# Expert tiles gather their rows by token number and add their outputs into a token-ordered sum

## What is computed

```
x = _layer_norm(DEEPNORM_ALPHA * x + mixed, ln_g[l, 0], ln_b[l, 0])
x = _layer_norm(DEEPNORM_ALPHA * x + grouped_moe(x, ...), ln_g[l, 1], ln_b[l, 1])

def grouped_moe(x, w_router, b_router, w_e_in, w_e_out):
    # best of 4 groups, then its 2 best experts of 4: expert (T, 2), weight (T, 2)
    flat_e = expert.reshape(-1)
    order = jnp.argsort(flat_e)
    tok = order // TOP_K
    h = lax.ragged_dot(xt[tok], w_e_in, group_sizes)      # 16 experts, 1024 -> 2 * 512
    h_gate, h_up = jnp.split(h, 2, axis=-1)
    y = lax.ragged_dot(jax.nn.silu(h_gate) * h_up, w_e_out, group_sizes)   # 512 -> 1024
    y = y * weight.reshape(-1)[order][:, None]
    return jnp.zeros_like(xt).at[tok].add(y)
```

## Time and profile before

| what | us |
|---|---|
| median of 3 runs (lowest, highest) | 3569.72 (3567.91, 3579.04) |
| span of the profiled execution, its own time | 3573.8 |
| layer 1: end of the mixer to the table | 1132 to 1255 |
| layer 1: table to the first product | 1255 to 1301 |
| layer 1: tile loop | 1301 to 1722 |
| layer 1: last eviction to the last bias | 1722 to 1802 |
| layer 2: the same four | 2910 to 3036, to 3082, to 3496, to 3569 |

### The profile page before, as it was taken

One profiled execution on the slowest core, in us unless ns is written; L12 is line 12 of the kernel. 1 busy time (PEld: TensorE's weight loads), 2 busy tenths in 40 slices (PEclk: granted clock), 3 DMA queues, 4 the chain that ended last, 5 costly groups with the idle time before them and its releaser, 6 DMA issues.

```text
span 3573.8 us, 47212 instructions
## 1 busy us (share of the span) xinstructions
PE 3068.0 (86%) x15514; PEld 1681.2 (47%) x15515; DVE 1576.8 (44%) x2553; ACT 1173.2 (33%) x1823; POOL 248.1 (7%) x146
## 2 busy tenths in 40 slices
PE   6899897899998749999378998968999986599992
PEld 4466555544444424544134666555444444244451
DVE  3333353423333348656633334534323323368666
ACT  3223302322221037656221233022222210367652
POOL 0000000000001240000400000000000012400005
PEclk8999896699999869999678997957999997799995
DMA  9200102021211079777511000020221120689764
GB/s 366 90 1 1 48 1 59 1 59 29 59 53 65 30 297 353 272 276 293 194 54 57 1 20 29 1 59 1 59 56 32 53 68 27 241 327 374 306 249 165
DMA packets 197713, 422.18 MB, mean 118 GB/s; under 512 B 13700, under 2 KB 99888, under 8 KB 196752
## 3 DMA queue, kind: packets, MB, share of 16 engines
q1 hardware_dynamic: 174112, 328.65, 26.2%
q10 hardware_dynamic: 13552, 55.58, 3.9%
q0 software_dynamic: 9920, 36.29, 2.8%
HBM read 352.31 MB, written 72.35 MB: 119 GB/s over the span
## 4 chain that ended last, share of the span: by engine, by line
PE 66%; issue 11%; DVE 7%; PEld 4%; ACT 3%; DMA 3%; POOL 2%; DVEq 1%; POOLq 1%; SPq 1%; PEldq 1%; ACTq 0%
PE PA L1724 14%; PE PB L1743 7%; PE PA L1394 6%; PE PA L1395 6%; PE PA L1396 6%; PE PB L1395 3%; PE PB L1394 3%; PE PB L1396 3%; PE PC L1375 2%; PE PB L1488 1%; PE PB L1594 1%; PE PD L1515 1%; PEld PA L1394 1%; POOLq L509 1%; POOL RC L510 1%
## 5 line engine op out<-in xcount | busy, mean ns | idle before, releaser
L1724 PE MATMUL PA<-XT,RA 128*128 128x512 f16 x2304 | 511.2, 382 | 36.7 <-DVE RA L879 33.0
L1724 PEld LDWEIGHTS PA<-XT,RA 128*128 128x128 f16 x2304 | 226.8, 99 | 303.4 <-issue 42.1
L879 DVE SCALAR_TENSOR_TENSOR XT<-OT,XT 128x1024 f16<-128x1024 f32 x256 | 300.1, 1245 | 105.8 <-ACT XT L770 105.8
L770 ACT ACTIVATE XT<-OT 128x1024 f16<-128x1024 f32 x256 | 247.7, 1045 | 150.1 <-DMA OT<-in_w_e_in_dram 108.0
L1394 PE MATMUL PA<-XT,W 128*128 128x512 f16 x704 | 268.7, 382 | 13.9 <-ACT WK L733 5.8
L1395 PE MATMUL PA<-XT,W 128*128 128x512 f16 x704 | 268.8, 382 | 0.0
L1396 PE MATMUL PA<-XT,W 128*128 128x512 f16 x704 | 268.5, 381 | 0.0
L1743 PE MATMUL PB<-W,WK 128*128 128x512 f16 x1152 | 260.1, 383 | 8.6 <-DVE W L879 5.7
L879 DVE SCALAR_TENSOR_TENSOR W<-W 128x512 f16<-128x512 f32 (+2 forms) x288 | 177.5, 659 | 171.7 <-ACT W L582 159.6
L1394 PE MATMUL PA<-W,XT 128*128 128x512 f16 (+1 forms) x640 | 237.7, 371 | 13.8 <-DVE W L879 12.8
L1395 PE MATMUL PA<-W,XT 128*128 128x512 f16 (+1 forms) x640 | 236.7, 370 | 0.0
(11 more groups left out here) (320 smaller groups left out, 4746.5 us busy)
## 6 DMA issues: line engine op xcount, KB each, us to landing
OT<-in_w_e_in_dram SPq DMA_DIRECT2D x256, 512.0 KB, 7.6
RA<-in_w_e_out_dram SPq DMA_DIRECT2D x128, 512.0 KB, 6.3
W<-in_w_in_dram SPq DMA_DIRECT2D x104, 512.0 KB, 6.2
RA<-rows SPq DMA_DIRECT2D x50, 512.0 KB, 5.4
rows<-WK ACTq DMA_DIRECT2D x48, 512.0 KB, 5.6
rows<-RA ACTq DMA_DIRECT2D x1, 16384.0 KB, 59.0
BR<-in_w_branch_dram SPq DMA_DIRECT2D x16, 512.0 KB, 6.9
W<-in_w_out_dram SPq DMA_DIRECT2D x16, 512.0 KB, 5.7
```

Of the source, the lines that this page charges most:

```text
L770: nc.scalar.activation(EIS[:, 0, k, :], WEI[:, k, :], ACT.Copy, scale=SW).then_inc(ei_hi, 1)
L879: return stt(dst, src, scale, high, ALU.mult, ALU.subtract)
L1724: q = mm(PA[:, half, :], ROWS[:, a, k * P:(k + 1) * P], EIS[:, b, k, half * HALF:(half + 1) * HALF], start=k == 0 and a + b == 0, stop=k = ...
```

## The change

The rows are no longer scattered to slots. Instead:

- SyncE stores each finished tile of `X1` to a token-ordered DRAM tensor `x1_rows`, whose last 128 rows are zero.
- Behind the table, VectorE and TensorE invert the slot numbers. For each of the 16 columns of slots, VectorE makes a one-hot of the rank in the tile (B) and of the tile, times token number and times weight (A); 16 float32 matmuls sum B-transposed times A. Out come `src_row` (for each row of each tile its token) and `row_wt` (its weight). Slots without a token point to padding rows.
- GpSimd gathers `ROW` of each tile by `src_row`, and for each tile adds the output rows, which ScalarE has scaled by `row_wt` at eviction, to `y_sum` by an accumulating indirect DMA. `y_sum` is in token order and is cleared at the end of the mixer by a DMA from `y_zero`, DRAM to DRAM, issued by GpSimd ahead of its first gain.
- SyncE's first weight load no longer stands behind the dispatch, and its loop holds weight loads only. After the last add it loads `y_sum` tile by tile, with four buffers.
- In the combine one VectorE instruction (`X1 * ALPHA + y`) takes the place of two, and GpSimd's alpha pass and gathers are gone.
- Small: `mem` is loaded by one DMA, the zeros written at the start are 9 + 1 tiles and not 32.

The diff, cut to its core (in order: GpSimd at the end of the mixer, GpSimd behind the table, ScalarE's eviction, VectorE and TensorE behind the table, VectorE in the combine):

```diff
+                    if t == 0:
+                        pool.wait_ge(zero_st, 32)
+                        pool.dma_start(y_sum, y_zero).then_inc(y_st, 16)
                     r = WK[:, (t % 2) * D:(t % 2 + 1) * D]
                     nc.gpsimd.tensor_tensor(r, r, lnp[0], ALU.mult)
...
-                for t in range(NT):
-                    for j in range(2):
-                        nc.gpsimd.indirect_dma_start(
-                            rows, bass.IndirectOffsetOnAxis(slots[:, j, t:t + 1], 0), X1[:, t, :], None
-                        ).then_inc(disp, 16)
-                pool.wait_ge(disp, at(disp, 2 * NT * 16))
-                for t in range(NT):
-                    nc.gpsimd.tensor_scalar(X1[:, t, :], X1[:, t, :], ALPHA, None, ALU.mult)
-                pool.wait_ge(y_st, (g0 + n_tiles + 1) * 16)
-                for t in range(NT):
-                    pool.wait_ge(y_used, at(y_used, t + 1))
-                    for j in range(2):
-                        nc.gpsimd.indirect_dma_start(
-                            OT[:, (2 * (t % 2) + j) * D:(2 * (t % 2) + j + 1) * D], None,
-                            rows, bass.IndirectOffsetOnAxis(slots[:, j, t:t + 1], 0)
-                        ).then_inc(y_ld[t % 2], 16)
+                def gather_tile(i):
+                    pool.wait_ge(row_tr, g0 + i + l)
+                    nc.gpsimd.tensor_copy(at_row[:, 0:1], src_row[:, bass.ds(i, 1)])
+                    pool.drain()
+                    gather(at_row[:, 0:1])
+                def add_rows(i):
+                    pool.wait_ge(y_ev, g0 + i + 2)
+                    nc.gpsimd.tensor_copy(at_row[:, 1:2], src_row[:, bass.ds(i, 1)])
+                    pool.drain()
+                    nc.gpsimd.indirect_dma_start(y_sum, bass.IndirectOffsetOnAxis(at_row[:, 1:2], 0), YROW, None,
+                                                 compute_op=ALU.add).then_inc(y_st, 16)
+                pool.wait_ge(x1_st, at(x1_st, NT * 16))
+                pool.wait_ge(inv_ok, at(inv_ok, 1))
+                gather(src_row[:, 0:1])
...
+                with pool.Fori(1, last) as i:
+                    gather_tile(i + 2)
+                    add_rows(i - 1)
+                add_rows(before_last)
+                add_rows(last)
...
-                    act.wait_ge(y_st, (g0 + i + 1) * 16)
-                    nc.scalar.activation(WK[:, 2048:3072], flat(PB), ACT.Copy, scale=UN).then_inc(y_ev, 1)
-                    act.drain()
-                    act.dma_start(rows[bass.ds(i * P, P), :], WK[:, 2048:3072]).then_inc(y_st, 16)
+                    act.wait_ge(y_st, (g0 + i) * 16 + (l + 1) * 16)
+                    nc.scalar.activation(YROW, flat(PB), ACT.Copy, scale=row_wt[:, bass.ds(i, 1)]).then_inc(y_ev, 1)
...
+                tt(A[:, :, TILES:2 * TILES], over(tile_f, TILES),
+                   co("iota128")[:, 0:TILES].unsqueeze(1).to_broadcast([P, 2 * NT, TILES]), ALU.is_equal)
+                tt(B, over(rank_f, P), co("iota128").unsqueeze(1).to_broadcast([P, 2 * NT, P]), ALU.is_equal)
+                tt(A[:, :, 0:TILES], A[:, :, TILES:2 * TILES], over(who, TILES), ALU.mult)
+                tt(A[:, :, TILES:2 * TILES], A[:, :, TILES:2 * TILES],
+                   over(m12[:, 2:4, :].rearrange("p j t -> p (j t)"), TILES), ALU.mult).then_inc(inv_a, 1)
+                v.wait_ge(inv_mm, at(inv_mm, 1))
+                ts(src_row[:, :], PC[:, 0, 0:TILES], co("tokid")[:, 0:1], 2.0 * T, ALU.add, ALU.add)
+                ts(row_wt[:, :], PC[:, 0, TILES:2 * TILES], UN, None, ALU.mult)
+                v.drain().then_inc(inv_ok, 1)
...
+                for i in range(2 * NT):
+                    q = mm(PC[:, 0, 0:2 * TILES], B[:, i, :], A[:, i, :], start=i == 0, stop=i == 2 * NT - 1)
+                q.then_inc(inv_mm, 1)
...
-                        stt(r, y1, m12[:, 2, t:t + 1], X1[:, t, :], ALU.mult, ALU.add)
-                        v.drain()
-                        stt(r, y2, m12[:, 3, t:t + 1], r, ALU.mult, ALU.add).then_inc(y_used, 1)
+                        stt(r, X1[:, t, :], ALPHA, OT[:, t % 4 * D:(t % 4 + 1) * D], ALU.mult, ALU.add
+                            ).then_inc(y_used, 1)
```

More of the change, by code:

```diff
@@ L107, in trunk @@
         mem_t = dram("mem_t", [P, 2 * KD * N_MEM], F16)
-        rows = dram("rows", [TILES * P, D])
+        x1_rows = dram("x1_rows", [T + P, D])
+        y_sum = dram("y_sum", [T + P, D])
+        y_zero = dram("y_zero", [T + P, D])
         keep_rate = dram("keep_rate", [LAYERS, BW])
@@ L210, in trunk @@
         par_ld = sem("par_ld", 6 * 16)
-        nat_ld = [sem(f"nat_ld{i}") for i in range(NT + MT)]
+        nat_ld = [sem(f"nat_ld{i}") for i in range(NT + 1)]
         bt_tr = sem("bt_tr", 1)
@@ L321, in trunk @@
         y_st = sem("y_st")
-        y_ld = [sem(f"y_ld{i}", 8 * 16) for i in range(2)]
+        y_ld = [sem(f"y_ld{i}", 2 * 16) for i in range(4)]
         y_used = sem("y_used", NT)
@@ L359, in _ @@
             sp.dma_start(CO[:, :], consts).then_inc(c_ld, 16)
[L360 to L365, removed]
+            for t in range(NT):
+                sp.dma_start(RC[:, t * D:(t + 1) * D], x[0, t * P:(t + 1) * P, :]).then_inc(nat_ld[t], 16)
+            sp.dma_start(OT[:, 0:MT * D].rearrange("p (t d) -> p t d", t=MT), mem[0].rearrange("(t p) d -> p t d", p=P)
+                         ).then_inc(nat_ld[NT], 16)
             sp.dma_start(hmask[:, :], chunk_mask).then_inc(misc_ld, 16)
@@ L419, in _ @@
                     sp.sem_inc(passed, 1)
-                for t in range(NT):
-                    sp.wait_ge(o_rd, at(o_rd, t + 1))
-                    sp.dma_start(xres[t % 2], out[0, t * P:(t + 1) * P, :]).then_inc(xr_ld[t % 2], 16)
+                for t in range(NT + 3):
+                    if t < NT:
+                        sp.wait_ge(o_rd, at(o_rd, t + 1))
+                        sp.dma_start(xres[t % 2], out[0, t * P:(t + 1) * P, :]).then_inc(xr_ld[t % 2], 16)
+                    if t >= 3:
+                        sp.wait_ge(o_x1, at(o_x1, t - 2))
+                        sp.dma_start(x1_rows[(t - 3) * P:(t - 2) * P, :], X1[:, t - 3, :]).then_inc(x1_st, 16)
                 sp.wait_ge(o_mm, at(o_mm, NT))
@@ L472, in _ @@
                 sp.dma_start(RA[:, 0:KD * N_MEM].bitcast(F16), mem_t).then_inc(mt_ld, 16)
+                sp.wait_ge(y_st, (g0 + last + 1) * 16 + (l + 1) * 16)
                 sp.sem_inc(passed, 1)
+                for t in range(NT):
+                    if t >= 4:
+                        sp.wait_ge(y_used, at(y_used, t - 3))
+                    sp.dma_start(OT[:, t % 4 * D:(t % 4 + 1) * D], y_sum[t * P:(t + 1) * P, :]).then_inc(y_ld[t % 4], 16)
             for i in range(4):
@@ L531, in _, with gather @@
-                for t in range(NT):
-                    pool.wait_ge(y_used, at(y_used, t + 1))
-                    pool.sem_inc(passed, 1)
-                    for j in range(2):
-                        nc.gpsimd.indirect_dma_start(
-                            OT[:, (2 * (t % 2) + j) * D:(2 * (t % 2) + j + 1) * D], None,
-                            rows, bass.IndirectOffsetOnAxis(slots[:, j, t:t + 1], 0)
-                        ).then_inc(y_ld[t % 2], 16)
-                    if t == 2:
-                        pool.wait_ge(ln2_ld, at(ln2_ld, 32))
-                    if t >= 2:
-                        gain(pool, l, t - 2)
+                def gather(column):
+                    nc.gpsimd.indirect_dma_start(ROW, None, x1_rows, bass.IndirectOffsetOnAxis(column, 0)
+                                                 ).then_inc(row_ld, 16)
@@ new lines, in _ @@
+                pool.sem_inc(passed, 1)
+                gather(src_row[:, 1:2])
+                pool.wait_ge(row_tr, g0 + (l + 2))
+                pool.sem_inc(passed, 1)
+                gather(src_row[:, 2:3])
+                with pool.Fori(1, last) as i:
[3 more added lines that the diff above has]
+                add_rows(last)
+                pool.wait_ge(ln2_ld, at(ln2_ld, 32))
+                for t in range(NT - 2):
+                    gain(pool, l, t)
@@ L1804, in constants @@
     put("ones", np.ones((P, P)))
[L1805 to L1807 removed]
     put("thr", np.tile(np.arange(8) * P, (P, 1)))
+    put("iota128", np.tile(np.arange(P), (P, 1)))
+    put("tokid", i[:, None] + P * np.arange(NT)[None, :] - T)
     return c, (same & (j_ <= i_)).astype(np.int32)
```

82 lines of the change are left out of this document (47 added, 35 removed).

## The result

| | median (lowest, highest), us | ratio to the kernel before, 95% interval |
|---|---|---|
| before | 3570.89 (3567.91, 3579.04), 4 runs | |
| after | 3551.65 (3550.95, 3556.59), 4 runs | 0.9947 [0.9933, 0.9961] |

The profiled execution's span is 3550.5 us, against 3573.8. The forecast, 3507 with a range of 3484 to 3545, gave the right sign and missed the size: about a third of the gain came. Each stage of a layer is cut here at the same marks, in the profiled executions: GpSimd's release at the mixer's end (its first gain pass, or the clear ahead of it), the cast of the table, the first and the last eviction of the tile loop, and VectorE's last scaling of the combine.

The account below looks back on a forecast made before the run. TensorE is two thirds of the chain, so only its idle stretches pay. Head 42.6, clear -1.4, loop -4, combine 3.5 and 22.2 sum to 62.9 off 3573.8: span 3510.9, median 3507 us, range 3484 to 3545.

Parts of the forecast that it names:

- the clear: Mixer's end: GpSimd's 4.7 MB DMA ahead of its first gain costs only its issue, 0.7 us a layer, 1.4 for both.
- the loop: Tile loop of both layers: a loss of 4 us in all, from the adds' extra bytes on full DMA engines.
- the start: Kernel start up to layer 1's GpSimd release: moved by 0; nothing costed for the zeros or the one mem load.
- the head: Table cast to first product: some 25.2 us against 46.5, a gain of 21.3 in each layer, 42.6.
- the combine: After the last eviction: first sum earlier by 3.4 and 0.1 us, then tiles in 45.0, gaining 13.5 and 8.7.
- Rival 4: Mixer's end: the clear holds GpSimd until it is copied, 2 x 19.1 us on TensorE's wait, 3545; chance 0.08.
- about 1.7, and its landing: Tile loop: an add needs 1.7 us for hand-over, index copy and issue, plus 8.0 landing: 9.7 of 15.85, hidden.
- the prediction's 1.28: Tile loop: an add moves 0.5 MB more than the store did, 1.28 us of the DMA engines at 410 GB/s.
- What would show the prediction wrong: ScalarE waiting for y_sum, weight chunks waited for in dense stretches beyond a few us, or the chain through the clear.
- the inversion's 7.06 us of matmuls: Head: 16 float32 matmuls, two weight loads of 0.22 us each, 7.0 us in all.
- the first weight DMA: Head: SyncE loads four registers first, so its first weight DMA is issued about 3 us after the cast.
- the hand-over: Last eviction's end to the combine's first sum: 13.6 us, from 1.7 + 8.0 for the add, 0.2, and 3.7 for the first load.

Follow-up runs that it names:

- run 2: Changed kernel, with a semaphore wait instead of the drain between GpSimd's first gain and bias passes, behind the clear: 3518.24 us.
- run 8: Kernel before, with GpSimd issuing a 4.7 MB DRAM copy to an unread buffer ahead of its first gain pass in each layer: 3601.74 us.
- run 3: Changed kernel with semaphore waits for both the tile loop's two GpSimd drains and the drain behind the clear: 3496.93 us.
- run 7: run 3 with the 512 KB of zeros for the padding rows of x1_rows issued by GpSimd, not ScalarE: 3489.86 us.
- run 5: run 3 with only the drain ahead of the gather put back: 3513.24 us.
- run 1: Changed kernel with semaphore waits instead of the tile loop's two GpSimd drains, ahead of gather and add: 3534.39 us.
- run 6: run 3 with only the drain ahead of the add put back: 3498.13 us.
- run 9: run 3 with ScalarE's last two start DMAs exchanged, the x1_rows zeros ahead of the 4.6 MB for y_zero: 3487.04 us.
- run 10: run 7 with a second add of the same rows into a second cleared buffer, the next eviction waiting for both: 3531.83 us.
- run 4: run 3 with rows scattered over y_sum without the accumulate: 3478.01 us; layer 2's routing came out with 23 tiles, not 24.

## Why the prediction was wrong

The spans: 3510.9 forecast, 3550.5 measured, 39.6 too low. By the table above: the clear 25.9 (14.3 and 11.6), the loop 17.4, the start 9.2, the head 2.5, less 10.9 that the combine gave beyond the forecast and 4.5 elsewhere.

**The step that failed is the same in two places:** the forecast costed what GpSimd issues, and not what stands next to it in GpSimd's program. "Its nearest row took 0.56 to issue ... I take the lower, since the issue row is for the same kind of instruction" was right on the issue (0.53). But behind the gain pass stood a drain, in the code before and after alike, and it turned the 17.5 us in which the copy lands into GpSimd's time. The sentence ahead of it, "whatever it costs GpSimd is paid in full", was right: the term of 1.4 us for both layers was 32 by run 2, of which 27 show against the kernel before, whose stretch was 1.0 and 3.5 us longer than run 2's. Rival 4 gave this cost (2 x 19.1) a chance of 0.08, by a mechanism that run 2 refutes: the DMA doesn't hold GpSimd, the drain does. Runs 2 and 8 show it from both sides.

In the loop, "about 1.7, and its landing", 9.7 of 15.85 and so hidden, took gather and add as independent. The add's landing (9.2 against 8.0 assumed) was hidden, as said, but the drain put the next gather behind it. Add and gather in a row don't fit: from the add's issue at 1369.27 to the next at 1388.20 are 18.9 us, where the loop's tile took 16.85 before. The 4 us that the text did book for the loop were for the engines' load, and no net loss shows: runs 3 and 7 have the loop of the kernel before within 0.5 us. The load itself is there. These are the loops of the kernel before, to be read against run 7's 0.83 and 0.85 above:

```profile
1342.00:1722.00 380.00, 374.00 (x1854) 185.97 (x1852) 247.62 (x234) 228.97 (x256) 0.00 (x0) 0.99 0.73 282
3120.00:3496.00 376.00, 373.12 (x1852) 185.70 (x1850) 255.83 (x242) 235.78 (x262) 0.00 (x0) 1.00 0.79 301
```

That is 38 and 23 us more of the engines, 1.3 a tile, as the prediction's 1.28 had it; it was wrong only in that TensorE would feel it. What would show the prediction wrong was named as ScalarE waiting for `y_sum`. It does, 45 to 93 us, in runs with and without the loss. The wait that went with the loss was TensorE's for the gather: 14.5 us in the changed kernel and 13.3 in run 5, none in runs 1, 3, 6 and 7. It is two thirds of the 21 us lost; the rest is not traced.

**The start** was costed at nothing ("for the zeros", whose bytes indeed land beside products). The small new DMA behind them was not looked at as an instruction of ScalarE; it cost some 9 us (runs 7 and 9).

**Right:** the head (25.97 against 25.2; the stage lost 19.8 and 20.3 us where 21.3 was forecast), the inversion's 7.06 us of matmuls, the first weight DMA 2.9 us after the cast (1281.66). **Mis-sized:** the hand-over, 10.6 us and not 13.6. The add's landing was taken at 8.0 and is 6.1 with no weights beside it; the issue and the first load were each 0.5 shorter. On this the fit that the prediction quoted from the Trainium skill, DMA: Bandwidth & Descriptors, section on the anatomy of one DMA, gave an estimated 4.4, 1.7 under the measured 6.08, where the 8.0 was 1.9 over. The rule of the Trainium skill, same page, section on issuing engines that are not separate DMA queues, that all issuers' DMAs share the same 16 engines, agrees with run 10's shares of 0.95; with a single add it didn't decide the time. And the combine's tiles took 42.9 and 42.3 us, not 45.0. The 4.9 us gained between the layers are not the change's: the kernel of run 8, which has the code of before there, shows 1107.0 in place of 1113.5.

With the drains out, run 3 is at 3496.93, inside the range, and 10 under the forecast. That it lies so near is in part luck: its span has the start 7.8 us over, against 7.9 under in the combines, 6.2 between the layers, 6.0 from release to cast and 4.1 in the loops.

## What to carry to other kernels

Ahead of any DMA that is added to an engine's program, read that program forward to the next instruction that waits for the engine's own past. A drain that costs next to nothing today takes on the landing time of each DMA put ahead of it; a semaphore raised by the one instruction that has to be done costs about the same here when nothing is under way (0.08 us between gain and bias against the drain's 0.15, 0.8 ahead of an indirect DMA against 0.9) and waits for nothing else. And where a wait is on a list of waits, try whether it moves the time before it is called the cause: ScalarE's on `y_sum` was 64.2 us with the loop's loss and 77.1 without it.

## What the runs showed of the hardware

- A drain of GpSimd waited for GpSimd's own DMAs (15.07 us behind a copy landing in 17.5, up to 8.9 and 7.6 us behind adds and gathers), and not for another queue's: SyncE issued a store of `X1` at 1161.83, which lands in 4.0 (median), and the drain of the second tile was through 0.15 us after the gain pass's end at 1164.10.
- An accumulating indirect DMA of 128 rows of 4 KB landed in 9.2 us (median, beside the weights) and in 6.1 with no weights beside it. By run 10 it takes the 16 engines 2.3 to 2.6 us, and by run 4 some 1.6 of that are the accumulate's; the profile counts 0.5 MB written for it and no read.
- GpSimd's issue of such a DMA takes 1.6 us as a rule, and 5.67 in one place where VectorE works on two SBUF operands at the same time:

```profile
1350.72 5.67 POOL L544 DMA_INDIRECT y_sum<-WK,at_row  x1 [0.92 <-issue]
...
1350.28 4.62 DVE L904 SCALAR_TENSOR_TENSOR W<-RA,W 128x1024 f16<-128x1024 f32 x4
```

  On this the Trainium skill, SBUF — State Buffer, section on who interferes with whom, says that a VectorE instruction with two SBUF inputs contends with a GpSimd instruction that reads SBUF; whether the issue of an indirect DMA counts as one it doesn't say. The row agrees in time and place, and in run 7 twelve of 48 such issues take 5.2 to 5.8 us, each beside at least 3.8 us of that VectorE work; no run here separates it from other causes.
- A DMA of 512 KB on ScalarE's queue took 9.96 us to issue behind one of 4.6 MB, and 0.59 ahead of it.
